# A two-layer decoder trunk on one core: the exchange of 32-row squares by way of memory off the chip

## What is computed

```python
def stick_breaking_layer(x, w_in, w_out):            # layer 0
    q, k, v, z = jnp.split(x @ w_in, 4, axis=-1)
    o = stick_breaking_attention(split_heads(q), split_heads(k), split_heads(v))
    return (merge_heads(o) * jax.nn.silu(z)) @ w_out

def moba_layer(x, w_in, w_out, k, v, k_mean, pos):   # layer 1
    q, z = jnp.split(x @ w_in, 2, axis=-1)
    o = moba_attention(rope(split_heads(q), pos), k, v, k_mean)
    return (merge_heads(o) * jax.nn.silu(z)) @ w_out

for i in range(DEPTH):                               # DEPTH = 2
    y = ...                                          # one of the two layers above
    x = layer_norm(DEEPNORM_ALPHA * x + y, ln_g[i], ln_b[i])
    x = x + (p[i] @ w_ple[i]) * jax.nn.sigmoid(x @ w_ple_gate[i])
```

## Time and profile before

| | |
|---|---|
| median of 3 runs | 1138.38 us (1137.45 to 1138.42) |
| profiled execution, its own time | 1139.46 us |
| its span, first to last instruction | 1137.8 us |
| TensorE busy | 1132.2 us, 5216 matmul instructions |
| VectorE, ScalarE, GpSimd busy | 754.9, 590.4, 266.0 us |
| moved by DMA | 238.82 MB, mean 210 GB/s |

### The profile page before, as it was taken

The page is one execution under the profiler, slowest core; times in us unless marked ns, Lnnn a source line. Parts: engine busy times, 40 slices in busy tenths (PEclk is TensorE's granted clock), DMA queues, the critical chain, the costliest instruction groups (busy, mean ns, idle before and its releaser), DMA issues.

```text
span 1137.8 us, 15463 instructions
## 1 busy us (share of the span) xinstructions
PE 1132.2 (100%) x5216; PEld 945.0 (83%) x5216; DVE 754.9 (66%) x811; ACT 590.4 (52%) x661; POOL 266.0 (23%) x539
## 2 busy tenths in 40 slices
PE   9999999999999999999999999999999999999998
PEld 8888888888888888888878888888888888888887
DVE  6665556556566566678888785557687777566863
ACT  6574556456547453455354555555455544435641
POOL 1402220330241300003437763420320312000000
PEclk9999999999999999999999999999999999999999
DMA  9876775675675686457687776765656768663671
GB/s 326 255 230 191 216 203 169 199 223 167 183 225 175 198 323 198 138 184 240 213 289 237 240 245 218 227 215 166 213 163 191 215 204 244 240 218 113 199 247 56
DMA packets 128635, 238.82 MB, mean 210 GB/s; under 512 B 14880, under 2 KB 17184, under 8 KB 128080
## 3 DMA queue, kind: packets, MB, share of 16 engines
q1 hardware_dynamic: 109888, 209.22, 59.1%
q0 software_dynamic: 18416, 28.52, 7.9%
q10 hardware_dynamic: 288, 0.52, 0.1%
HBM read 216.71 MB, written 4.19 MB: 194 GB/s over the span
## 4 chain that ended last, share of the span: by engine, by line
PE 90%; DVE 5%; DMA 3%; ACT 1%; issue 1%; POOL 1%; ACTq 0%; SPq 0%; DVEq 0%; POOLq 0%
PE acc L1240 28%; PE acc L1242 27%; PE acc L1241 27%; DMA raw<-in_w_ple_gate 2%; PE aux L1277 2%; DVE w_lo L772 2%; PE acc L1219 1%; PE aux L1303 1%; PE aux L1270 1%; DVE stage L967 1%; POOL stage L446 1%; DMA stage<-v_or_z 0%; DVE big L1006 0%; DVE v_or_z L1003 0%; DVE act L787 0%
## 5 line engine op out<-in xcount | busy, mean ns | idle before, releaser
L772 DVE TENSOR_TENSOR w_lo<-raw,w_hi 128x1024 fp32r<-128x1024 f32 x388 | 469.3, 1222 | 317.1 <-ACT w_hi L499 316.5
L499 ACT ACTIVATE w_hi<-raw 128x1024 fp32r<-128x1024 f32 x388 | 409.7, 1059 | 442.7 <-PE acc L1242 358.2
L1240 PE MATMUL acc<-w_hi,act 128*128 128x512 f32 x1532 | 600.3, 392 | 0.9 <-DVE act L787 0.8
L1242 PE MATMUL acc<-w_hi,act 128*128 128x512 f32 x1532 | 596.7, 389 | 0.0
L1241 PE MATMUL acc<-w_lo,act 128*128 128x512 f32 x1532 | 596.3, 389 | 0.0
L1242 PEld LDWEIGHTS acc<-w_hi,act 128*128 128x128 f32 x1532 | 287.6, 188 | 60.7
L1240 PEld LDWEIGHTS acc<-w_hi,act 128*128 128x128 f32 x1532 | 287.7, 188 | 60.2 <-DVE act L787 1.9
L1241 PEld LDWEIGHTS acc<-w_lo,act 128*128 128x128 f32 x1532 | 287.9, 188 | 58.2
L446 POOL DMA_DIRECT2D heads<-big x192 | 94.0, 498 | 274.8 <-DVE big L793 231.7
L446 POOL DMA_DIRECT2D heads<-heads x128 | 63.5, 504 | 129.0 <-DVE heads L1158 121.0
L446 POOL DMA_DIRECT2D heads<-v_or_z x64 | 31.3, 498 | 51.9 <-DVE v_or_z L793 39.1
(11 more groups left out here) (161 smaller groups left out, 659.1 us busy)
## 6 DMA issues: line engine op xcount, KB each, us to landing
raw<-in_w_in_a SPq DMA_DIRECT2D x124, 512.0 KB, 3.9
raw<-in_w_ple_gate SPq DMA_DIRECT2D x64, 512.0 KB, 4.8
raw<-in_w_in_b SPq DMA_DIRECT2D x64, 512.0 KB, 4.5
raw<-in_w_kv SPq DMA_DIRECT2D x64, 512.0 KB, 4.0
raw<-in_w_out_a SPq DMA_DIRECT2D x32, 512.0 KB, 4.8
raw<-in_w_out_b SPq DMA_DIRECT2D x32, 512.0 KB, 5.7
heads<-big POOLq DMA_DIRECT2D x192, 32.0 KB, 3.3
heads<-in_ln_rows POOLq DMA_DIRECT2D x4, 1024.0 KB, 9.9
```

Of the source, the lines that this page charges most:

```text
L499: nc.scalar.activation(w_hi[:, r], raw[:, r % RAWS], ACT.Copy).then_inc(hi_ready, 1)
L772: nc.vector.tensor_tensor(w_lo[:, r], raw[:, r % RAWS], w_hi[:, r].bitcast(F32), ALU.subtract) \
L1240: nc.tensor.matmul(dst, hi, w_hi[:, r, i], start=begin, stop=False)
L1242: mm = nc.tensor.matmul(dst, lo, w_hi[:, r, i], start=False, stop=end)
```

## The change

An exchange no longer moves squares within SBUF. GpSimd issues one DMA that writes the whole turned buffer, 128 rows of 4 KB (6 KB for probabilities), to one of four scratch tensors in HBM, waits until that has landed, and issues four DMAs that read it back. Each of the four reads 32 rows and lays their four parts of 1 KB on the four groups of partitions. The readers wait for 64 instead of 256. Two steps change place in the first chunk after layer 0: `last_x2_hi` goes from behind ScalarE's split of piece 3 to behind that of piece 2; on VectorE `last_x2_lo` goes ahead of the split of piece 3, and `find_shift(1)` from behind the split of piece 2 to behind that of piece 3. TensorE makes ten warm-up products instead of nine.

```diff
-WARM_UPS = 9
+WARM_UPS = 10
 SQUARE = 32
-MOVED = 16 * (P // SQUARE) ** 2
+MOVED = 16 * (P // SQUARE)
...
+        bounce = [nc.dram_tensor(f"bounce{i}", [P, 4 * SC], F32).ap() for i in range(4)]
...
+        bounced = sem("dma_bounced")
...
+            turn, bounces = itertools.count(0), itertools.count(1)
+
             def exchange(turned, count, dst, src, moved, width=HT // NS):
 
                 pool.wait_ge(turned, count)
+                through = bounce[next(turn) % len(bounce)]
+                pool.dma_start(through[:, 0:NS * width], src[:, 0:NS * width]).then_inc(bounced, 16)
+                pool.wait_ge(bounced, 16 * next(bounces))
                 for a in range(NS):
-                    for g in range(NS):
-                        pool.dma_start(dst[g * SQUARE:(g + 1) * SQUARE, a * width:(a + 1) * width],
-                                       src[a * SQUARE:(a + 1) * SQUARE, g * width:(g + 1) * width]) \
-                            .then_inc(moved, 16)
+                    rows = through[a * SQUARE:(a + 1) * SQUARE, 0:NS * width].rearrange("i (g w) -> g i w", g=NS)
+                    pool.dma_start(dst[:, a * width:(a + 1) * width], rows).then_inc(moved, 16)
...
-            pieces(N_Q, N_Q, {3: [last_x2_hi, lambda: normalise_x2(0)]})
+            pieces(N_Q, N_Q, {2: [last_x2_hi], 3: [lambda: normalise_x2(0)]})
...
-            pieces(N_Q, N_Q, {2: [lambda: find_shift(1)], 3: [last_x2_lo, lambda: normalise_x2(0)],
-                              4: [lambda: turn_normed(0)]} | q_end(0, 0), before={0: [lambda: x2_lo(G - 2)]})
+            pieces(N_Q, N_Q, {3: [lambda: find_shift(1), lambda: normalise_x2(0)],
+                              4: [lambda: turn_normed(0)]} | q_end(0, 0), before={0: [lambda: x2_lo(G - 2)], 3: [last_x2_lo]})
```

More of the change, by code:

```diff
@@ L16 @@
+import itertools
 import math
```

## The result

The changed kernel takes 1171.37 us (median of 6 runs, 1166.11 to 1177.67) against 1138.4 (1137.16 to 1139.43): a ratio of 1.0297, interval 1.0274 to 1.0321. It is slower by 33 us, where the forecast was a gain of 0.8 us and the range ended at 1141.0.

The account below looks back on a forecast made before the run. TensorE, busy nearly throughout, was taken as the bound. Reordering -0.98, warm-up +0.22 and exchange 0 summed to -0.76 us against the profiled execution's 1139.46, or 1137.6 us against the median 1138.38; range 1136.6 to 1141.0.

Parts of the forecast that it names:

- The bound: Whole kernel: TensorE is busy in 1132.2 of 1137.8 us; at most 0.98 us to gain, no such bound on loss.
- The reordering: First chunk after layer 0: running `last_x2_lo` earlier removes TensorE's one stall, -0.98 us.
- The warm-up: Kernel start: a tenth warm-up delays the first real product by 0.43 us, of which 0.22 us is lost.
- The length of the new exchange: Each exchange through HBM: write, wait, issues and last landing take 8.9 to 15.9 us, 12.0 in between.
- The covers and their limits: Time before TensorE waits: new exchanges may take 13.1 us for keys, 15.3 for probabilities, 13.8 for x2; all expected under.
- The x2 chain: Gate stage, last quarter of x2, ahead of piece 4: cover 0.8 us, limit 13.8 us, exchange expected at 13.5 us.
- More traffic: Exchanges' bytes move twice, +17.3 MB on 238 MB; hidden by eight split pieces ahead of TensorE, so 0 us.
- Rival B: Keys and probabilities: round trip outlasts the covers, 1143.6 us at 1 us over both, up to 1153; 17%.

Follow-up runs that it names:

- back_by_group: The changed kernel with its four reads cut by destination group, each laying 128 memory rows of 1 KB on 32 partitions: 1148.51 us, ratio 1.0100.
- out_by_group: The changed kernel with the rearrangement on the way out, four writes of 32 partitions each, then one read of whole rows: 1138.77 us, ratio 1.0004.

## Why the prediction was wrong

- **The bound.** Right. TensorE sets the time, a gain of 0.98 us was all there was, and a loss had no such bound.
- **The reordering.** Right in its mechanism: the wait is gone. The 0.98 us are inside the interval of the measurement and can't be confirmed as a size. In the changed kernel it had no effect that can be told, since the chain ahead of it was late.
- **The warm-up.** Delay of the first product right (0.43 said, 0.44 seen); its price depends on when the pace rises, which differs between executions, and I had one profile.
- **The length of the new exchange: the step that failed.** The sum was out + 0.1 + 1.7 + last landing. For keys I took 5.8 + 0.1 + 1.7 + 4.4 = 12.0; the second group's has 5.1 + 0.3 + 2.0 + 7.2 = 14.6. For probabilities I took 14.0 with 5.5 for the last landing; the four have 17.4 to 18.0, with a last landing of 10.8 to 11.4, far outside the 6.4 that I had set as the end of the bound. The out leg was mostly sized too long (4.0 to 4.3 us for probabilities where I took 6.7). The last landing was mis-sized for two reasons. I priced a read of 128 KB by another read of 128 KB and looked at bytes and piece size, not at the shape of the address pattern, where each engine's share is a quarter of the transfer and not a sixteenth. And I priced one read, not the last of four beside the weights: with the shape mended, in back_by_group, the last landing is still 5.3 to 6.6 us for keys and 8.1 to 8.9 for probabilities.
- **The covers and their limits.** For probabilities right: 17.8, 18.0 and 17.4 us against 15.3, and TensorE waited 2.4, 2.6 and 2.0. For keys the limit of 13.1 us was held to be fixed, and the change itself moved it to 12.2 to 12.6, by way of the queries' exchange, to which I had given no price; the first group's 2.3 us came from late weights. The x2 chain was right as a place but not as a mechanism: I had the delay of an exchange as its cause and up to 1 us of late weights on top, and the record shows 5.6 us more of waiting for weights in the stage and 1.1 us more for the exchange; and it met TensorE at the transposes before it met piece 4.
- **More traffic.** Right for the bytes: out_by_group carries them all at a ratio of 1.0004. Wrong for the way in which the changed kernel moves them: I put the term at nothing because the splits run eight pieces ahead of TensorE, but the keys' copies and the sigmoids stand behind splits in ScalarE's order, and a late weight piece reaches TensorE through them. 6.0 of the 21.1 us of waits are mostly of this kind (the first group's keys, 2.3, and x2, 3.7).
- **Rival B** was the case that came true, with 17%. Its upper end, 1153, was still too low for three reasons: the last landing, the late weights, and what no row of the kernel before could show since TensorE never stopped there, that a wait can be followed by a slow stretch. Of the span's 31 us, 20 are waits and 10.5 are clock.
- **The range** ended at 1141 because I let B begin at 1 us over the limits, where the price is six times that. This kernel had 0.98 us to win and three chains to lose at; the range had to reach into B, and the chance of slower had to be larger with all three limits only 0.3 to 1.3 us away.

## What to carry to other kernels

Before replacing many small DMAs by a few larger ones, read the outer dimension of each new address pattern: a read with 4 in front kept a quarter of the engines busy, and 512 KB in reads with 32 in front on both sides landed 2 us sooner, with nothing else moving. When the main engine is full, work out the limit of each chain first and compare it with the new duration's upper bound, not its middle; and ask what else the change delays that the limit itself rests on, as the queries and the weights did here. And count a wait of the matrix engine at more than its length: here 20 us of waits brought 10 more of slow clock.

## What the runs showed of the hardware

- A read of 128 KB in pieces of 1 KB landed after 2.4 us with one group in front, 5.4 with two, 3.3 to 4.0 with four, 2.8 with eight and 2.3 with sixteen. While the data moved, the busy share of the 16 engines was 0.11, 0.26 and 0.41 with two, four and eight. GpSimd's time to issue them goes the same way, 0.57, 0.83, 0.71, 0.59 and 0.53 us.
- Writing 512 KB to HBM in rows of 4 KB takes 2.9 us alone and 4.7 beside the weights (median of 31, four of them of 768 KB), less than the 7.2 us median of the spill's writes before.
- Sixteen transfers within SBUF take 9.0 and 9.8 us alone, nearly all of it issue; one write and one read of whole rows with nothing rearranged take 2.9 + 3.8 us.
- The granted clock fell to 0.50 about one microsecond after a wait of 2.38 us had ended and stayed there for some three; it did not fall after waits of 0.9, 1.7 and 2.44 us, and it fell after one of 1.86.
- Beside reads of 1 KB pieces from HBM the slowest landing of a 512 KB weight piece in the gate stage was 10.6 to 11.6 us; it was 9.1 in the kernel before and 8.9 where the small pieces were writes.
